# One sparse layer's norms on another engine, attention steps further apart, and a last MLP in token order

## The reference, cut to what matters

```python
def masked_softmax(logits, mask):
    logits = jnp.where(mask, logits, NEG)
    m = jnp.max(logits, axis=-1, keepdims=True)
    e = jnp.where(mask, jnp.exp(logits - m), 0.0)
    return e / jnp.maximum(jnp.sum(e, axis=-1, keepdims=True), 1e-30)
...
def sq_relu_mlp(h, w_up, w_down):
    return jnp.square(jax.nn.relu(h @ w_up)) @ w_down
...
    for l in range(DEPTH_2):
        h = rmsnorm(x, g_attn[l])
        if l < N_A_LAYERS:
            x = x + dsa_mixer(...)
        else:
            x = x + nsa_mixer(...)
        x = x + sq_relu_mlp(rmsnorm(x, g_mlp[l]), w_up[l], w_down[l])
...
    return rmsnorm(x, g_final)
```

## Time and profile before

| what | value |
|---|---|
| median of three runs | 1811.7 us |
| the profiled execution | 1811.6 us |
| its span in the profile | 1810.0 us |
| TensorE (PE) busy | 1673.0 us, 92% |
| VectorE (DVE) busy | 1076.6 us, 59% |
| ScalarE (ACT) busy | 832.4 us, 46% |
| GpSimd (POOL) busy | 462.2 us, 26% |
| the three attention stages, first scores to last output | about 52, 32 and 50 us |
| last matmul of the second MLP to the end of the span | 20.6 us |

### The profile page before, as it was taken

How to read it: one execution, slowest core, us unless ns; L and a number is a source line. 1 busy time by engine, 2 the same in 40 slices (tenths; PEclk the granted TensorE clock), 3 DMA queues, 4 the chain that set the end, 5 groups by cost and what they waited for, 6 DMA issues and landing times.

```text
span 1810.0 us, 34218 instructions
## 1 busy us (share of the span) xinstructions
PE 1673.0 (92%) x11384; PEld 1510.8 (83%) x11384; DVE 1076.6 (59%) x2473; ACT 832.4 (46%) x1768; POOL 462.2 (26%) x415
## 2 busy tenths in 40 slices
PE   5975889999999999999999999789999898899996
PEld 3872689998999999878788777589999857699996
DVE  5537569935777751565656566855556524765554
ACT  3213445664444444555555542455555213555552
POOL 4111367886666678100000004010000000010000
PEclk8975799999999999999999998899999997999999
DMA  8861134554444445555655553145555462055552
GB/s 310 320 214 47 59 129 152 175 177 136 139 139 140 139 145 181 185 194 188 193 189 193 189 189 104 35 129 185 180 181 174 140 215 76 13 164 184 179 182 93
DMA packets 80753, 287.63 MB, mean 159 GB/s; under 512 B 10081, under 2 KB 11409, under 8 KB 80433
## 3 DMA queue, kind: packets, MB, share of 16 engines
q1 hardware_dynamic: 72016, 257.30, 43.3%
q0 software_dynamic: 7344, 26.35, 3.9%
q10 hardware_dynamic: 1328, 3.15, 0.5%
HBM read 284.14 MB, written 2.62 MB: 158 GB/s over the span
## 4 chain that ended last, share of the span: by engine, by line
PE 82%; DVE 9%; ACT 3%; issue 2%; DMA 2%; POOL 1%; SPq 0%; DVEq 0%; ACTq 0%; POOLq 0%
PE pu L544 12%; PE pu L545 12%; PE pu L546 12%; PE pacc L601 6%; PE pacc L603 6%; PE pacc L602 6%; PE pacc L545 3%; PE pacc L544 3%; PE pacc L546 3%; PE pu L516 2%; PE pu L526 2%; PE pacc L648 2%; PE pm L817 2%; PE pn L817 2%; POOL ring_lo L359 1%
## 5 line engine op out<-in xcount | busy, mean ns | idle before, releaser
L352 ACT ACTIVATE ring_hi<-ring 128x512 fp32r<-128x512 f32 x880 | 505.6, 622 | 525.1 <-PE pu L546 288.5
L359 DVE TENSOR_TENSOR ring_lo<-ring,ring_hi 128x512 fp32r<-128x512 f32 x592 | 385.9, 694 | 335.3 <-ACT ring_hi L352 335.1
L544 PE MATMUL pu<-Xh,ring_hi 128*128 128x256 f32 x1472 | 431.0, 293 | 24.3 <-DVE Xl L1415 5.3
L545 PE MATMUL pu<-Xl,ring_hi 128*128 128x256 f32 x1472 | 419.5, 285 | 0.0
L546 PE MATMUL pu<-Xh,ring_lo 128*128 128x256 f32 x1472 | 419.3, 285 | 0.0
L359 POOL TENSOR_TENSOR ring_lo<-ring,ring_hi 128x512 fp32r<-128x512 f32 x288 | 370.6, 1309 | 130.2 <-ACT ring_hi L352 129.6
L544 PEld LDWEIGHTS pu<-Xh,ring_hi 128*128 128x128 f32 x1472 | 285.1, 194 | 30.3 <-issue 18.1
L545 PEld LDWEIGHTS pu<-Xl,ring_hi 128*128 128x128 f32 x1472 | 285.9, 194 | 0.2
L546 PEld LDWEIGHTS pu<-Xh,ring_lo 128*128 128x128 f32 x1472 | 285.2, 194 | 0.0
L601 PE MATMUL pacc<-ring_hi,vh 128*128 128x512 f32 x512 | 200.4, 391 | 0.0
L603 PE MATMUL pacc<-ring_lo,vh 128*128 128x512 f32 x512 | 200.3, 391 | 0.0
(11 more groups left out here) (358 smaller groups left out, 2627.2 us busy)
## 6 DMA issues: line engine op xcount, KB each, us to landing
ring<-in_weights SPq DMA_DIRECT2D x488, 512.0 KB, 3.3
big<-in_ada POOLq DMA_DIRECT2D x40, 512.0 KB, 6.4
bias_row<-big ACTq DMA_DIRECT2D x1, 1536.0 KB, 6.8
XT<-in_xT ACTq DMA_DIRECT2D x1, 1024.0 KB, 8.4
scr<-in_ada POOLq DMA_DIRECT2D x2, 512.0 KB, 12.4
tk<-in_ada POOLq DMA_DIRECT2D x2, 512.0 KB, 14.1
early_h<-in_ada POOLq DMA_DIRECT2D x2, 512.0 KB, 16.1
early_l<-in_ada POOLq DMA_DIRECT2D x2, 512.0 KB, 17.6
```

Of the source, the lines that this page charges most:

```text
L352: nc.scalar.activation(ring_hi[:, n % 2, half], ring[:, n % RING, half], ACT.Copy).then_inc(s["split_hi"], 1)
L359: api.tensor_tensor(ring_lo[:, n % RING, half], ring[:, n % RING, half], ring_hi[:, n % 2, half], ALU.subtract).then_inc(s[LOW[name][0]], 1)
L544: mm(out, ring_hi[:, n % 2, w], xh, start=start, stop=False, skip_group_check=True)
L545: mm(out, ring_hi[:, n % 2, w], xl, start=False, stop=False, skip_group_check=True)
```

## The change

1. **Steps further apart.** In all three attentions PE does transposes(st-3) and products(st-4), ACT copies(st-3) and outs(st-5).
2. **DSA.** POOL adds bias and choice of keys into `Sb[u % 4]` ahead of time (semaphores `chosen`, `att_prebias`; it waits for the exponential of unit u-4). DVE then has one add where it had two.
3. **NSA.** DVE makes only the reciprocal; POOL multiplies the probabilities by it and by the gate (`att_inverse`).
4. **Second MLP.** Its down slots run in token order (`token_slot`); no clearing by zeros, but `residual_rows` puts `XT` into `pacc` by 16 f32 products with the identity, after the first four up slots. No `close_acc`. The last slot (`last_rows`) does all of the first 128 tokens, then all of the second.
5. **The end.** For each half of the tokens: ACT squares 1024 columns with a row sum and takes the root of one column; DVE takes its reciprocal and multiplies two halves of 512 columns by the final gain `fin_row`; SP writes each of the four pieces by itself (256 KB). `fin_row` is loaded by POOL's queue during the second MLP, 4 KB spread over all partitions.
6. **The start.** The first 16 modulation rows share a semaphore in pairs.

```diff
@@ the attention on PE
-                for step in range(u0, u1 + 3):
+                for step in range(u0, u1 + 4):
                     if step < u1:
                         scores(step)
-                    if u0 <= step - 2 < u1:
-                        transposes(step - 2)
                     if u0 <= step - 3 < u1:
-                        products(step - 3)
+                        transposes(step - 3)
+                    if u0 <= step - 4 < u1:
+                        products(step - 4)
@@ the attention on ACT
-                for st in range(u0, u1 + 4):
+                for st in range(u0, u1 + 5):
                     if st < u1:
                         exps(st)
-                    if u0 <= st - 2 < u1:
-                        copies(st - 2)
-                    if u0 <= st - 4 < u1:
-                        outs(st - 4)
+                    if u0 <= st - 3 < u1:
+                        copies(st - 3)
+                    if u0 <= st - 5 < u1:
+                        outs(st - 5)
@@ POOL
+            u0, u1 = SPAN["dsa"]
+            for u in range(u0, u1):
+                tt, h = UNITS[u][1:3]
+                L = keys_of(u)
+                pool.wait_ge(s["chosen"], tt + 1)
+                if u >= u0 + 4:
+                    pool.wait_ge(s["att_exp"], u - 3)
+                nc.gpsimd.tensor_tensor(Sb[:, u % 4, 0:L], Bt[:, h, T - L:T], selb[:, tt, 0:L], ALU.add)\
+                    .then_inc(s["att_prebias"], 1)
             add_squares("mlp0")
+            pool.wait_ge(s["gates_done"], 1)
+            for u in range(*SPAN["nsa"]):
+                _, tt, h, b = UNITS[u][:4]
+                pool.wait_ge(s["att_inverse"], u + 1 - SPAN["nsa"][0])
+                pr = Pb[:, u % 4, 0:keys_of(u)]
+                nc.gpsimd.tensor_scalar(pr, pr, stats[:, 8 + u % 4:9 + u % 4], gates[:, tt, 3 * h + 1 + b:3 * h + 2 + b],
+                                        ALU.mult, ALU.mult).then_inc(s["att_normed"], 1)
             add_squares("mlp1")
+            pool.wait_ge(s["slots_used"], SLOT["mlp1"])
+            pool.dma_start(fin_row[:, :], fin_row_d.partition_broadcast(P)).then_inc(s["weights_row_loaded"], 16)
@@ DVE, DSA
-                step(v.tensor_tensor(S, ps, Bt[:, h, T - L:T], ALU.add))
-                v.tensor_tensor(S, S, selb[:, tt, 0:L], ALU.add).then_inc(s["att_biased"], 1)
+                dve.wait_ge(s["att_prebias"], u - SPAN["dsa"][0] + 1)
+                v.tensor_tensor(S, ps, S, ALU.add).then_inc(s["att_biased"], 1)
@@ PE, second MLP
+            def residual_rows(product):
+
+                for c in range(C):
+                    pe.wait_ge(s["evacs"], USE[product] + c + 1)
+                    for tt in range(TT):
+                        at0 = tt * D + c * P
+                        mm(paccf[:, at0:at0 + P], XT[:, c, tt * P:(tt + 1) * P], ident[:, :], start=(c % 4 == 0), stop=False,
+                           skip_group_check=True)
+
+            def last_rows(name, k):
+
+                n = SLOT[name] + k
+                for tt in range(TT):
+                    rows = slice(tt * P, (tt + 1) * P)
+                    xh, xl = act_h[:, k % 4, rows], act_l[:, k % 4, rows]
+                    for half, w in enumerate(halves):
+                        out = paccf[:, tt * D + half * 512:tt * D + (half + 1) * 512]
+                        split_ready(name, k, half, None)
+                        mm(out, xh, ring_hi[:, n % 2, w], start=False, stop=False, skip_group_check=True)
+                        mm(out, xl, ring_hi[:, n % 2, w], start=False, stop=False, skip_group_check=True)
+                        last = mm(out, xh, ring_lo[:, n % RING, w], start=False, stop=True, skip_group_check=True)
+                    last.then_inc(s["rows_done"], 1)
@@ ACT, the end
-            act.wait_ge(s["x_ready"], 4)
-            squares(XT[:, :, :], sq[:, :, :])
-            root(NORM["fin2"])
+            act.wait_ge(s["roots"], NORM["mlp1"])
+            for tt in range(TT):
+                act.wait_ge(s["rows_done"], tt + 1)
+                f(scratch[:, tt, :], paccf[:, tt * D:(tt + 1) * D], ACT.Square,
+                  accum_out=stats[:, tt:tt + 1]).then_inc(s["row_squares"], 1)
+                act.wait_ge(s["row_squares"], tt + 1)
+                f(stats[:, 4 + tt:5 + tt], stats[:, tt:tt + 1], ACT.Sqrt, scale=1.0 / D, bias=eps[:, 0:1])\
+                    .then_inc(s["row_roots"], 1)
@@ DVE, the end
-            dve.wait_ge(s["acc_done"], 3)
-            v.tensor_tensor(XT[:, :, :], pacc[:, :, :], XT[:, :, :], ALU.add).then_inc(s["x_ready"], 1)
-            dve.wait_ge(s["x_ready"], 4)
-            scaled(sq, XT, [column("fin2", c) for c in range(C)], NORM["fin2"]).then_inc(s["out_ready"], 1)
+            def rows_out(tt):
+
+                dve.wait_ge(s["row_roots"], tt + 1)
+                step(v.reciprocal(stats[:, 8 + tt:9 + tt], stats[:, 4 + tt:5 + tt]))
+                for half in halves:
+                    v.scalar_tensor_tensor(out_rows[:, tt, half], paccf[:, tt * D + half.start:tt * D + half.stop],
+                                           stats[:, 8 + tt:9 + tt], fin_row[:, half], ALU.mult, ALU.mult)\
+                        .then_inc(s["out_ready"], 1)
```

More of the change, by code:

```diff
@@ L192, in build @@
         ssum = R[:, T:2 * T]
+        fin_row = sb("fin_row", [P, D], F32, where["Xh"])
+        scratch = sb("scratch", [P, TT, D], F32, where["Xl"])
+        out_rows = sb("out_rows", [P, TT, D], F32, where["sq"])
         def area_r(name, *dims):
@@ L945, in mlp @@
                     up_slot(name, k, USE[name] + k, None, 4, None, raw_x[name])
-                four_down(None)
-                with pe.Fori(1, FF // P // 4) as g:
+                if name == "mlp1":
+                    residual_rows("b_o")
+                for k in range(4, 8):
+                    down(name, k, None)
+                with pe.Fori(1, FF // P // 4 - (name == "mlp1")) as g:
                     for k in range(4):
                         up_slot(name, k, USE[name] + k, g, 4, None, raw_x[name])
-                    four_down(g)
-                close_acc()
+                    for k in range(4, 8):
+                        down(name, k, g)
+                if name == "mlp0":
+                    close_acc()
+                else:
+                    k0 = 2 * FF // P - BODY
+                    for k in range(k0, k0 + 4):
+                        up_slot(name, k, USE[name] + k // BODY * 4 + k % 4, None, 4, None, raw_x[name])
+                    for k in range(k0 + 4, k0 + 7):
+                        down(name, k, None)
+                    pe.wait_ge(s["act_tiles"], 2 * FF // P)
+                    last_rows(name, k0 + 7)
             mlp("mlp0")
@@ L1026, in _ @@
             mlp("mlp1")
-            norm_sum("fin2")
         @block.scalar
@@ L1428, in scaled, with attend @@
                 return last
-            def attend(kind, bias, gate=None, filler=None):
+            def attend(kind, bias, filler=None):
                 u0, u1 = SPAN[kind]
@@ L1447, in normed @@
                     dve.wait_ge(s["att_exp"], u + 1)
-                    step(v.reciprocal(stats[:, 8 + u % 4:9 + u % 4], stats[:, 4 + u % 4:5 + u % 4]))
-                    L = keys_of(u)
-                    pr = Px[:, u % 4, 0:L]
-                    if gate is None:
-                        last = v.tensor_scalar(pr, pr, stats[:, 8 + u % 4:9 + u % 4], None, ALU.mult)
-                    else:
-                        last = v.tensor_scalar(pr, pr, stats[:, 8 + u % 4:9 + u % 4], gate(u), ALU.mult, ALU.mult)
-                    last.then_inc(s["att_normed"], 1)
+                    inverse = v.reciprocal(stats[:, 8 + u % 4:9 + u % 4], stats[:, 4 + u % 4:5 + u % 4])
+                    if kind == "nsa":
+                        inverse.then_inc(s["att_inverse"], 1)
+                        return
+                    step(inverse)
+                    pr = Px[:, u % 4, 0:keys_of(u)]
+                    v.tensor_scalar(pr, pr, stats[:, 8 + u % 4:9 + u % 4], None, ALU.mult).then_inc(s["att_normed"], 1)
                 for st in range(u0, u1 + 1):
@@ L1900, in _ @@
                 L = (tt + 1) * P
-                last = v.tensor_scalar(selb[:, tt, 0:L], work[:, tt, 0:L], -2.0e38, NEG, ALU.is_gt, ALU.mult)
-            step(last)
-            dve.wait_ge(s["bias_ready"], 1)
+                v.tensor_scalar(selb[:, tt, 0:L], work[:, tt, 0:L], -2.0e38, NEG, ALU.is_gt, ALU.mult)\
+                    .then_inc(s["chosen"], 1)
             def dsa_bias(u, S, ps):
@@ L2010, in _ @@
             step(v.tensor_scalar(gates, gates, 1.0, None, ALU.add))
-            step(v.reciprocal(gates, gates))
+            v.reciprocal(gates, gates).then_inc(s["gates_done"], 1)
+            dve.wait_ge(s["gates_done"], 1)
             dve.wait_ge(s["cmp_psum"], 1)
@@ L2125 @@
         "keys": np.concatenate([a["peer_keys_1"][0].T, a["peer_keys_2"][0].T], axis=1),
-        "rel_bias": a["rel_bias_2"], "bucket_onehot": onehot, "sinks": a["swa_sinks"][0],
```

(1 more changed line is left out.)

47 lines of the change are left out of this document (27 added, 20 removed).

## The result

The changed kernel takes 1789.85 us, the median of four runs (1788.88 to 1794.43), beside 1812.2 us for the kernel before: a ratio of 0.9884, 95% interval 0.9859 to 0.9909. Measured again with the experiments it takes 1792.3 us (five runs, 1791.67 to 1798.28) beside 1810.4 us: 0.9906 (0.9889 to 0.9923).

What follows compares the result with a forecast made beforehand. Most of the run was taken as PE matmul stages left alone, with PE or loops limiting the attentions and a serial end. Terms -0.5, 0, -3.2, -0.3 and -13.5 summed to -17.5 us from 1811.7: 1794 us, range 1787 to 1800.

Steps and rivals of the forecast that it cites:

- Steps further apart, windowed attention, -0.5: Windowed attention: PE is full, so only small waits around the modulation rows go; -0.5 us (0 to -1.5).
- Steps further apart, NSA, 0: NSA: the loop through ACT's copy stays at 3.24 us a pair, so 0 for 32 units.
- the bound of 12: NSA: most that steps further apart could gain, from PE's own work of 2.53 us a pair; -12 us at most.
- The rival of a faster NSA: NSA speeds up as well, as freeing the norm may loosen the copy; half the bound, 1788 us; chance 0.12.
- NSA's norm on POOL, 0: NSA: POOL's multiplication, priced from a 0.99 us row, hides up to about 1.5 us; 0 in all.
- DSA's early add, -3.2: DSA: the add removed from DVE is in the loop, 0.33 or 0.46 us a pair; -3.2 us (-1.5 to -5).
- the clock comes up sooner: Second attention: fewer PE holes raise the clock earlier, 1792 us; 1785 if the first attention rises too; chance 0.06.
- The second MLP, -0.3: Second MLP: token-order slots -4.3 us, residual products +4.1, dropped zero products 0; sum -0.3 (+0.7 to -1.5).
- The end, -13.5: After the last product: 7.1 us (6 to 8.5) to the span's end instead of 20.6; -13.5 us (-12 to -14.6).
- The start, 0: Kernel start: paired modulation rows delay the first by one landing, while DVE waits anyway for small loads; 0.
- POOL is dearer: NSA's long half: at 2.0 us a unit POOL's norm becomes the bound, +6 us, 1800 us; chance 0.08.
- the case slower than before: NSA: POOL's norm at 2.5 us a unit loses all 17.5 us; at 2.8, 1820 us; chance 0.01 to 0.02.

Runs made afterwards that it cites:

- the copy ahead: Changed kernel with ACT copying turned probabilities of unit v-3 before the exponential of unit v in all three attentions: 1778.5 us, ratio 0.9818.
- the tripled norm: Changed kernel with POOL's norm in NSA preceded by two more multiplications of the same form that nobody reads: 1803.7 us.

## Why the prediction came out right

The forecast was 1794.0 (1787 to 1800). The medians, 1789.9 and 1792.3, are inside the range. By the ledger the stages that the terms speak of fell by 19.8 us, not 17.5; chance elsewhere gave 0.4 back.

- **Steps further apart, windowed attention, -0.5:** 53.04 to 53.24, nothing. In the window that I read PE was full at half clock, and slack gives a full engine nothing. Not all of the stage is like that: the copy ahead takes 1.1 us off it (52.11).
- **Steps further apart, NSA, 0:** right, and for the reason given. The pairs stay at 3.24 us, products wait for ACT, transposes for nobody, exactly as the last part of the prediction asked. The copy ahead of the exponential shows that the loop was the right one: cut it and the stage loses 11.5 us, near the bound of 12. The rival of a faster NSA did not occur: -0.5 in the ledger, with the norm in it. I took the wait for the norm as slack that simply goes; it belongs to a second loop, a little shorter than the first. And the rival's "within 0.2 us" was misread: the norm was done by 1564.33 and the copy at 1564.66.
- **NSA's norm on POOL, 0:** right (0.2 to 0.8 us). The price was wrong: 0.55 us, not the 0.99 of the nearest row.
- **DSA's early add, -3.2:** -3.7 (and -4.8 in the first profile). The pairs came out as said, 2.84 for 2.85 and 3.25 for 3.25, and with both adds back they are 3.17 and 3.7 again. That the totals lie so close is in part luck, for two terms were off and nearly cancel.

  One is the clock. PEclk is 0.84 in the window from 1158 to 1162, first line below this list, where before it stood at 0.50 up to 1166, second line, and two pairs of 256 keys that had taken 4.1 to 4.2 us took 3.4 and 2.9 (3.0 and 2.9 in the first profile), about 1.1 us less than the add explains. So the rival "the clock comes up sooner" did happen, in DSA, while the windowed attention stayed at 1.2 GHz.

  The other is the end of the stage. From the scores that open its last pair to the first slot of the projection it takes 12.27 us instead of 12.05, where I had counted a gain of about 1. The greater distance, with a third transposition behind the last scores, costs 0.67 there (12.27 for 11.60 with the early add, 12.73 for 12.06 without), and the add gives 0.46.

  The distance also has a part in the clock, which is back at full 20.5 us behind the first scores before, 13.6 with the distance alone, 13.9 with the add alone, and 13.1 and 10.7 with both. The Trainium skill ("TensorE: Matmul & The Clock Gate", Part 1, on the two states) has the clock at full after a sustained busy stretch. Busy time did not foretell it here: before, PE was busy for 12.77 of the 14 us from 1152 to 1166, at 0.50 all along, and in the change it had been busy for only 4.41 of the 6 us from 1152 to 1158 when the clock rose (the last two lines below the list).
- **The second MLP, -0.3:** -1.5. (The terms -4.3 and +4.1 make -0.2.) Residual 3.5 us, not 4.1: I took 0.13 us a record from a row of products with a switch to them; it is 0.11. Slots 2.73 us in the mean, not 2.75, where one had taken 2.88: 0.6 more over 32. The clearing by zeros stood ahead of the sum and its absence gained 0.5 there; the wait for the squared tiles grew from 1.35 to 1.81 us, as the term "0" for the zeros said.
- **The end, -13.5:** -14.3. 6.35 us instead of 7.1. ACT, root, reciprocal and multiplications came out as in the working (1780.92 to 1784.7, 3.8 for 3.7); the last write landed in 2.1 us, not 3.0. That is the mis-sized term, and it lay in its range of 2.0 to 3.9.
- **The start, 0:** the first scores come at 146.46 for 146.38.

DSA, PE alone, in the changed kernel and in the kernel before:

```profile
1158.00:1162.00 4.00, 3.09 (x17) 0.84 0.02 4
```
```profile
1162.00:1166.00 4.00, 3.63 (x12) 0.50 0.00 0
```

The busy time ahead of the rise, in the same order:

```profile
1152.00:1158.00 6.00, 4.41 (x16) 0.50 0.00 1
```
```profile
1152.00:1166.00 14.00, 12.77 (x41) 0.50 0.01 2
```

The rival "POOL is dearer" and the case slower than before were right in their form, as the tripled norm showed, and far from the real price: 0.55 us where they needed 2.0 and 2.5.

## What to carry to other kernels

Read a pipelined stage as loops, not as shares: follow one unit from its first instruction to the instruction that it holds up, over every engine's program order, and count the units that this loop spans. When the ends of two waits lie within a few tenths of a us of each other, there may be two loops of nearly the same length, and an edit that opens one of them is worth little until the other is opened; it is then worth a lot (here 0.2 and 0.4 us alone, 11.6 together). An instruction that is ready early (a copy) should stand ahead of one that ends the newest unit's chain (an exponential) in the program order of its engine.

## What the runs showed of the hardware

- POOL multiplies 128x256 f32 by two columns in 0.55 us (128x128: 0.45), where DVE takes 0.41 (0.35) for the same in the kernel with NSA's norm back on DVE, while a multiplication by one column took 0.99 in the kernel before. These rows differ in tile and place as well; no run here tells which of them makes the difference.
- POOL's early adds beside DVE in DSA did not slow DVE's multiplication as the filling of memory had the earlier trace rows. Line 1521 of the changed kernel, window 1145:1180, has a median of 0.35 us and at most 0.45:

```profile
L1521 DVE TENSOR_SCALAR big<-big,stats x16: 286/352/449, 1152.0 to 1172.4; 128x128 f32<-128x128 f32 x8, 128x256 f32<-128x256 f32 x8
```

- Behind waits of 1.45, 2.46, 2.81 and 1.81 us (the norm behind the windowed attention, the slots behind DSA and behind NSA, the second MLP) PE goes on at full clock in some executions and at half clock for most of 4 us in others, with the same code. Each time costs 1.2 to 2.5 us.
- The clock also falls with no wait ahead of it, in runs of narrow products (24 and 15 columns, PE busy for 2.00 of 2.00 us), and sooner in some executions than in others: 2.9 us there between the two profiles of the change.
